# Router logits in four column groups, the routing chain in another order, the first expert weights split meanwhile, and another end of the program

## What is computed

```python
def moe_ffn(h, router, w1, w3, w2):
    shape = h.shape
    ht = h.reshape(-1, shape[-1])
    logits = (ht @ router).astype(jnp.float32)
    top_v, top_i = lax.top_k(logits, TOP_K)
    wts = jax.nn.softmax(top_v, axis=-1)
    combine = jnp.sum(jax.nn.one_hot(top_i, N_EXPERTS, dtype=jnp.float32) * wts[..., None], axis=1).astype(h.dtype)

    def expert_step(acc, p):
        e1, e3, e2, cw = p
        return acc + cw[:, None] * swiglu(ht, e1, e3, e2), None
    ...
# at the end of the layer:  x = x + gt2 * rms_norm(ffn(h), g_post_ffn[l])
```

## Time and profile before

| | |
|---|---|
| three timed executions | 2008.66, 2008.34 and 2004.48 us, median 2008.34 |
| the profiled execution's own time | 2004.63 us, its span 2002.5 us (2.1 us lie around the span) |
| TensorE | busy 94% of the span, mean granted clock 0.95 of full speed |
| VectorE, ScalarE, GpSimd | busy 62%, 53%, 2% |
| chain that ended last | TensorE 84%, VectorE 9%, ScalarE 3%, DMA 2%, issue 2% |
| the expert part | from about 1058 us to the end |

### The profile page before, as it was taken

One profiled execution on the slowest core, in us unless ns is written; L12 is line 12 of the kernel. 1 busy time (PEld: TensorE's weight loads), 2 busy tenths in 40 slices (PEclk: granted clock), 3 DMA queues, 4 the chain that ended last, 5 costly groups with the idle time before them and its releaser, 6 DMA issues.

```text
span 2002.5 us, 25665 instructions
## 1 busy us (share of the span) xinstructions
PE 1889.0 (94%) x10248; PEld 1547.4 (77%) x10248; DVE 1244.3 (62%) x1416; ACT 1071.2 (53%) x1432; POOL 32.0 (2%) x33
## 2 busy tenths in 40 slices
PE   6999879999999999998797999999999999999995
PEld 3877456898888787975586888888888888888783
DVE  3332751552232336434645989898888989898886
ACT  4323542462222226434436777767676777676764
POOL 0000000000000000000000110000000000000000
PEclk9999885899999999998877999999999999999997
DMA  8211643222322221414513999999989999998983
GB/s 345 101 48 70 234 159 127 83 69 102 105 84 105 85 106 50 147 64 183 218 64 145 368 351 361 348 360 347 360 344 355 351 342 365 337 371 335 355 335 148
DMA packets 61531, 441.87 MB, mean 221 GB/s; under 512 B 6836, under 2 KB 6964, under 8 KB 8288
## 3 DMA queue, kind: packets, MB, share of 16 engines
q1 hardware_dynamic: 60032, 436.23, 58.1%
q10 hardware_dynamic: 1120, 3.28, 0.4%
q0 software_dynamic: 256, 0.66, 0.1%
HBM read 439.10 MB, written 1.05 MB: 220 GB/s over the span
## 4 chain that ended last, share of the span: by engine, by line
PE 84%; DVE 9%; ACT 3%; DMA 2%; issue 2%; SPq 0%; ACTq 0%; DVEq 0%
PE psum L1610 73%; PE psum L2002 2%; DMA raw<-units 2%; PE psum L1849 1%; PE psum L1855 1%; PE psum L2045 1%; DVE row_max L1260 1%; PE psum L1627 1%; PE psum L2018 1%; ACT probs L870 1%; DVE w_lo L1116 1%; PE psum L1633 1%; DVE states L1291 1%; DVE act_lo L1180 1%; DVE probs L1254 1%
## 5 line engine op out<-in xcount | busy, mean ns | idle before, releaser
L1495 DVE TENSOR_TENSOR w_lo<-raw,w_hi 128x2048 fp32r<-128x2048 f32 x136 | 311.0, 2290 | 50.6 <-ACT w_hi L1014 49.9
L1014 ACT ACTIVATE w_hi<-raw 128x2048 fp32r<-128x2048 f32 x136 | 260.8, 1919 | 106.3 <-PE psum L1610 104.7
L1116 DVE TENSOR_TENSOR w_lo<-raw,w_hi 128x1024 fp32r<-128x1024 f32 x130 | 153.2, 1220 | 188.8 <-ACT w_hi L671 188.7
L1610 PE MATMUL psum<-w_hi,xt_hi 128*128 128x512 f32 x596 | 233.4, 392 | 2.7 <-DVE xt_lo L1500 2.7
L1610 PE MATMUL psum<-w_hi,xt_lo 128*128 128x512 f32 x596 | 232.7, 390 | 0.0
L1610 PE MATMUL psum<-w_lo,xt_hi 128*128 128x512 f32 x596 | 232.4, 390 | 0.0
L1495 DVE TENSOR_TENSOR w_lo<-raw_more,w_hi 128x2048 fp32r<-128x2048 f32 x90 | 206.0, 2290 | 34.5 <-ACT w_hi L1014 34.2
L1610 PE MATMUL psum<-act_hi,w_hi 128*128 128x512 f32 (+1 forms) x608 | 218.6, 359 | 1.4 <-DVE w_lo L1116 1.3
L1610 PE MATMUL psum<-act_hi,w_lo 128*128 128x512 f32 (+1 forms) x608 | 217.9, 358 | 0.0
L1610 PE MATMUL psum<-act_lo,w_hi 128*128 128x512 f32 (+1 forms) x608 | 217.9, 358 | 0.0
L1014 ACT ACTIVATE w_hi<-raw_more 128x2048 fp32r<-128x2048 f32 x90 | 172.7, 1919 | 74.4 <-PE psum L1610 74.4
(11 more groups left out here) (273 smaller groups left out, 3509.5 us busy)
## 6 DMA issues: line engine op xcount, KB each, us to landing
raw<-units SPq DMA_DIRECT2D x295, 1024.0 KB, 4.8
raw_more<-units SPq DMA_DIRECT2D x120, 1024.0 KB, 4.9
X<-ctx_in ACTq DMA_DIRECT2D x1, 1024.0 KB, 16.8
X<-x_in ACTq DMA_DIRECT2D x1, 1024.0 KB, 23.5
out<-X SPq DMA_DIRECT2D x1, 1024.0 KB, 4.1
const<-const_in ACTq DMA_DIRECT2D x1, 520.0 KB, 10.0
rope<-rope_in POOLq DMA_DIRECT2D x2, 256.0 KB, 5.4
wsm<-wsm_in ACTq DMA_DIRECT2D x1, 288.0 KB, 27.5
```

Of the source, the lines that this page charges most:

```text
L1014: act.activation(w_place(m)[0], raw_place(m), ACT.Copy).then_inc(esem("w_high"), 1)
L1116: ins = dve.tensor_tensor(w_lo[:, i % RING, part], raw[:, i % RING, part], w_hi[:, i % RING, part].bitcast(F32), ALU.subtract)
L1495: dve.tensor_tensor(lo, raw_place(m), hi.bitcast(F32), ALU.subtract).then_inc(esem("w_ready"), 1)
L1610: ins = pe.matmul(dst, lhs(a), rhs(b), start=first and n == 0, stop=last and n == 2)
```

## The change

Six things, all in the expert part:

1. The logits are made with the router's weights as the stationary operand (padded to 32 columns, in four column groups of the array, key `LR`); ScalarE copies the four partial sums, and a product with a 0/1 matrix (`C_SUM`) adds and turns them (`LG`). The router's weights in SBUF grow from 64 to 256 columns.
2. VectorE instead of ScalarE makes the last half tile of `h2T` (`last_half`), and its clearing of `y_moe` comes behind that. A one-element Exp on ScalarE (`warm`) stands ahead of the tokens' rounding.
3. VectorE makes two of the four lower parts of the tokens behind `routed`. ScalarE's copies of the gates move behind the split of unit 1, and its splits no longer wait for the places.
4. VectorE splits only units 0 and 1 ahead of the first gathered tokens, and ScalarE only 0, 1 and 2; the first up chunk waits for each half of the gathered tokens apart.
5. A down chunk makes all of its first 512 columns and then all of the second, and signals in between (`out_half`) in a pass's last chunk; `output` takes the halves apart. The last pass's `output` stands at the end of `run`, ahead of the `If`, and the split of the unit that is three beyond the run's end stands inside the `If`.
6. The end is made by halves of 512 columns on VectorE and ScalarE alone: `finish` squares and gates each half as soon as it is added, the root's function is loaded ahead, GpSimd's sum is gone, and the two tiles are stored apart.

```diff
-            out += [("LG",)] + [("H2", q) for q in range(4)] + [("GB", l, 1, 1, h) for h in range(2)] + [("POS",)]
+            out += [("LR",), ("H2", 0), ("LG",)] + [("H2", q) for q in range(1, 4)] + [("GB", l, 1, 1, h) for h in range(2)] + [("POS",)]
...
@@ sync @@
-        for t in token_tiles(1, "out"):
+        for n, t in enumerate(token_tiles(1, "out")):
             sp.wait_ge(x_added("ffn", 1, t), 1)
-        sp.dma_start(out[0].rearrange("(t p) d -> p t d", p=P), X[:, CTX // P:TILES, :]).then_inc(stored, 16)
-        sp.wait_ge(stored, 16)
+            sp.dma_start(out[0, n * P:(n + 1) * P, :], X[:, t, :]).then_inc(stored, 16)
+        sp.wait_ge(stored, 32)
...
@@ scalar @@
+        copy_out(("LR",), mod_row[:, :], bank(("LR",))[:, 0:256])
+        act.activation(warm[:, :], eps, ACT.Exp).then_inc(sem("exp_table"), 1)
         for q in range(4):
...
-        gates_on_all(1, 1, (1,))
         act.wait_ge(sem("top_gap"), 1)
         act.activation(rt[:, 4:6], rt[:, 4:6], ACT.Exp).then_inc(sem("top_exp"), 1)
-
-        wait_copied(act, ("POS",))
...
-            wait_used(act, ("down", p * FC + FC - 1))
             if p:
                 act.wait_ge(esem("scattered"), 4 * p)
             for h in range(2):
+                if h == 0:
+                    act.wait_ge(esem("out_half"), p + 1)
+                else:
+                    wait_used(act, ("down", p * FC + FC - 1))
...
-                if down is not None:
+                if down is not None and down != run_last(r):
                     high(ahead(("down", down)))
                 if c == GATHER_STEP and p + 1 < PASSES_OF:
                     columns_high(p + 1)
+            output(RUNS[r][-1])
...
                 act.wait_ge(sem("xn_mix1"), TILES)
+                columns_high(0)
             high(m)
-        columns_high(0)
+            if m == 1:
+                gates_on_all(1, 1, (1,))
         run(0)
+
+        def finish(p):
+
+            act.activation(std[:, 0:1], eps, ACT.Sqrt).then_inc(sem("root_table"), 1)
+            for n in range(4):
+                tt, h = divmod(n, 2)
+                act.wait_ge(esem("added"), 4 * p + n + 1)
+                if n >= 2:
+                    act.wait_ge(sem("final_square"), n - 1)
+                act.activation(y_junk[:, h * 512:(h + 1) * 512], y_moe[:, tt, h * 512:(h + 1) * 512], ACT.Square,
+                               accum_out=y_part[:, 2 + tt, h:h + 1]).then_inc(sem("final_square"), 1)
 
         def extra(k):
             with act.If(run_valid(act, k)):
+                high(RUN_END[k] + W_RING - 1)
                 run(k + 1)
...
@@ vector @@
+        tokens_low(0)
+        tokens_low(1)
         dve.wait_ge(sem("top_exp"), 1)
...
         dve.sem_inc(sem("routed"), 1)
+        tokens_low(2)
+        tokens_low(3)
...
-        for m in range(W_RING):
-            low(m)
+        low(0)
+        low(1)
         columns_low(0)
+        low(2)
+        low(3)
         run(0)
 
+        def gated_half(n):
+
+            tt, part = n // 2, slice((n % 2) * 512, (n % 2 + 1) * 512)
+            dve.wait_ge(sem("final_square"), n + 1)
+            dve.tensor_tensor(y_moe[:, tt, part], y_moe[:, tt, part], gate[:, 1, 1, part], ALU.mult).then_inc(
+                sem("final_gate"), 1)
+
         def finish(p):
-            output(p)
-            for n in range(4):
-                added(p, n, n)
-            dve.wait_ge(esem("added"), 4 * p + 4)
-            dve.sem_inc(sem("summed"), 1)
+            added(p, 0, 0)
+            added(p, 1, 1)
+            added(p, 2, 2)
+            dve.wait_ge(esem("added"), 4 * p + 4 - 1)
+            gated_half(0)
+            added(p, 3, 3)
+            gated_half(1)
...
+        tile_sum(0, 2)
+        gated_half(2)
+        tile_out(0, 2)
+        tile_sum(1, 3)
+        gated_half(3)
+        tile_out(1, 3)
...
@@ tensor @@
-        for tt in range(2):
-            for k in range(KT):
+        for k in range(KT):
+            for tt in range(2):
                 wait_copied(pe, ("TT", 1, "ffn", tt, k // 4))
-                ins = pe.matmul(bank(key)[:, tt * EXPERTS:(tt + 1) * EXPERTS], h2T(k)[:, tt * P:(tt + 1) * P],
-                                wsm[:, 512 + k * EXPERTS:512 + (k + 1) * EXPERTS], start=k == 0, stop=k == KT - 1)
+            group = slice(32 * (k % 4), 32 * (k % 4 + 1))
+            ins = pe.matmul(bank(key)[group, 0:LAT], wsm[:, 512 + 32 * k:512 + 32 * (k + 1)], h2T(k),
+                            start=k < 4, stop=k >= 4)
...
-            if c == 0:
-                pe.wait_ge(esem("xt_lo"), 2 * p + 2)
...
             for i in range(2):
+                if c == 0:
+                    pe.wait_ge(esem("xt_lo"), 2 * p + i + 1)
...
-            for j in range(2):
-                for h in range(2):
+            for h in range(2):
+                for j in range(2):
...
+                if c == FC - 1 and h == 0:
+                    ins.then_inc(esem("out_half"), 1)
```

More of the change, by code:

```diff
@@ L290 @@
 A_WSM = A_COLS + N_COLS
[L291 removed]
+WSM = 512 + 32 * KT
+A_GW2 = A_WSM + WSM
 A_AM = A_GW2
@@ L653, in _ @@
                     select(extra)
-        add(1, "ffn", y_moe_of)
     @block.scalar
@@ L800, in seam @@
                     tile_modulated(*after, n - 1, tiles[n - 1], (1,))
-            tile_modulated(*after, len(tiles) - 1, tiles[-1])
+            tile_modulated(*after, len(tiles) - 1, tiles[-1], (0,) if after == (1, "ffn") else (0, 1))
         def gate_logs(l):
@@ L1057, in run @@
                     high(ahead(("up", up, 0)))
-                    if c == (2 if p < EXPERTS else 0) and p:
+                    if c == 2 and 0 < p < EXPERTS:
                         output(p - 1)
@@ L1084, in extra @@
                 else:
-                    output(EXPERTS + k)
+                    finish(EXPERTS + k)
             with act.Else():
-                output(EXPERTS + k - 1)
+                finish(EXPERTS + k - 1)
         extra(0)
-        act.wait_ge(sem("summed"), 1)
-        mean_square("post", 1, "ffn", (2, 3), y_moe_of, lambda t: y_junk[:, :], lambda n: None)
+        for n, t in enumerate(token_tiles(1, "out")):
+            act.wait_ge(sem("final_sum"), n + 1)
+            act.activation(y_std[:, t:t + 1], y_ssq[:, t:t + 1], ACT.Sqrt, bias=eps, scale=1.0 / D_MODEL).then_inc(
+                sem("final_std"), 1)
     @block.vector
@@ L1371, in seam, with last_half @@
                     tile_low(*after, n - 1, tiles[n - 1], (1,))
+            if after == (1, "ffn"):
+                last_half(len(tiles) - 1, tiles[-1])
             tile_low(*after, len(tiles) - 1, tiles[-1])
+        def last_half(n, t):
+            key = ("TT", 1, "ffn", n, 1)
+            dve.wait_ge(sem("scale1"), 8)
+            dve.wait_ge(sem("turned_ffn1"), 2 * n + 2)
+            for k in range(4, KT):
+                ins = dve.tensor_scalar(h2T(k)[:, (t - 2) * P:(t - 1) * P], bank(key)[:, (k % 4) * P:(k % 4 + 1) * P],
+                                        modc[:, 1, 4, k, 1:2], modc[:, 1, 3, k, 1:2], ALU.mult, ALU.add)
+            empties(ins, key)
         def out_projection(l):
@@ L1467, in _, with tokens_low @@
         dve.tensor_tensor(field(TAKEN), field(FIRST), field(SECOND), ALU.add).then_inc(sem("taken"), 1)
-        for q in range(4):
+        def tokens_low(q):
             key = ("H2", q)
@@ L1974, in _ @@
             ins.then_inc(filled, 1)
+        tokens_back(0)
+        key = ("LG",)
+        wait_copied(pe, ("LR",))
+        wait_emptied(pe, key)
+        for tt in range(2):
+            ins = pe.matmul(bank(key)[:, tt * EXPERTS:(tt + 1) * EXPERTS], mod_row[:, tt * P:(tt + 1) * P],
+                            const[:, C_SUM:C_SUM + EXPERTS], start=True, stop=True)
+        ins.then_inc(filled, 1)
+        for q in range(1, 4):
+            tokens_back(q)
         gates_on_all(1, 1, (1,))
@@ L1986, in _ @@
         wait_copied(pe, ("POS",))
+        for q in range(4):
+            wait_copied(pe, ("H2", q))
         def gather(p):
```

37 lines of the change are left out of this document (22 added, 15 removed).

## The result

| | median of 4 timed executions | lowest to highest |
|---|---|---|
| before | 2006.41 us | 2003.92 to 2008.66 |
| after | 1984.89 us | 1981.62 to 1987.86 |

The ratio of after to before is 0.989, with a 95% interval of 0.987 to 0.991: faster, by 21.5 us. The forecast was 1992.0 us with a range of 1986 to 1998.

The account below looks back on a forecast made before the run. TensorE was taken as busy almost throughout, leaving gains only at the front and end: 7.2 + 7.7 - 0.3 = 14.6 us. That gave 1990.0 from the profiled execution, 1993.7 from the median; middle 1992.0, range 1986.0 to 1998.0.

Parts of the forecast that it names:

- selection earlier, behind the mark: Before the gather: `routed` at 1069.2 instead of 1073.96, 4.8 us earlier; the mark is the start of the last tile's turning.
- gather to first up product: Front: gather from 1071.1 at half clock throughout, with its two turnings, first up matmul at 1078.4; 7.3 us.
- more half clock in the up products: First up products: half clock may last somewhat longer since no pause precedes them; 0.5 us taken off.
- front: Everything ahead of the first up matmul: 7.2 us gained, after taking off 0.5.
- between: Expert passes: nothing from the new column order; 0.3 us lost to the router's padded weights in an early load.
- last down matmul to first sum: Kernel's end: first sum at 1981.6 instead of 1984.10, the `If` again costing 3.5 us; 2.5 us gained.
- end: Everything behind the last down matmul: 6.4 us from sums and finish plus 1.3 from the halved final store, 7.7 us.
- The second rival: Gather: the clock stays up through it, 3 to 4 us more gained, 1988.5 us; chance 0.2.
- the third rival: Kernel's end: the short branch over other `Else` bodies stalls like the long one, 3 us, 1995 us; chance 0.07.
- the clock rival: Gather: full clock kept through it, 3 to 4 us more gained, 1988.5 us, range down to 1986; chance 0.2.
- The GpSimd rival: Selection: VectorE's splits hold up GpSimd, `sel` 2.3 or 4.6 us later, 1994.3 to 1996.6 us; chance 0.25.
- the one on the order within down chunks: Down chunks: six matmuls in a row into one bank cost more, slower from 16 ns each; 2022 at 25 ns; chance 0.02.

Follow-up runs that it names:

- e1: The kernel before, unchanged, run again; ratio to before 0.9994 (0.9985 to 1.0002).
- e4: The kernel after, unchanged, run again; ratio to before 0.9895 (0.9877 to 0.9913).
- e6: The kernel after with VectorE's first split moved ahead of the tokens' last two lower parts, beside the selection; ratio to before 0.9931.
- e10: The kernel after with the product of a run's last up chunk ahead of the split of its second unit; ratio to before 0.9900.
- e11: The kernel after with the split that no pass uses back ahead of the last output and the `If`, on both engines; ratio to before 0.9905.
- e12: The kernel after with gates behind places and the product of a run's last up chunk ahead of the split; 1982.93 us, ratio to before 0.9889.
- e2: The kernel before with only the front of the change (items 1 to 4), the end as before; ratio to before 0.9944.
- e7: The kernel after with the last pass's output inside the `Else` and in the next run's start, not ahead of the `If`; ratio to before 0.9918.
- e8: The kernel after with four extra products of 256 columns, result unused, in TensorE's pause ahead of the gather; ratio to before 0.9895.
- e9: The kernel after with the gates' eight products moved behind the places' products on TensorE, into the pause before the gather; ratio to before 0.9904.

## Why the prediction was off

The sum was 14.6 us; the two totals give 20.0, and timed executions 20.2 (e1's median against e4's) to 22.0 (the median of all 17 executions of before on that chip against e4's). By its steps:

| step (bold: us gained) | predicted | measured | |
|---|---|---|---|
| selection earlier, behind the mark | 4.8 | 5.2 | logits 2.26 us where 2.0 were put; the chain behind a little shorter |
| gather to first up product | 7.3 us | 5.83 us | 1.5 us at full clock |
| more half clock in the up products | -0.5 | 0 | half clock in them: 2.9 us before, 2.5 after |
| **front** | 7.2 | 9.6 | |
| **between** | -0.3 | 0.4 | half of it by the up products' clock |
| last down matmul to first sum | 2.5 less | 3.7 less | 8.47 to 4.79 us |
| four sums | 4.55 us | 4.19 us | 4.59 before |
| last sum to `X` complete | 5.35 us | 4.71 us | 9.22 before |
| release of the store to the end | 3.3 us | 3.1 us | 4.59 before |
| **end** | 7.7 | 10.1 | |

**Front.** The step that failed is "It took 7.2 us with its two turnings, at half clock throughout; the last ends at about 1078.4": 5.83 us were measured. The second rival, the clock that stays up through the gather, happened in part. Against it stood that small products do not raise the clock; but it rose 9.0 us behind the mark, in the turnings back, and fell at 15.6 to 15.8 (after; e4, e6, e10, e11 and e12 alike). Before it rose at 12.1 and fell at 19.0, just ahead of the gather at 19.5. The change brought the gather to 14.3, in front of the fall. The prediction took the clock as a property of the gather, and the rival as all or nothing, so that its middle had no place in the forecast. Why the clock falls at that moment stays open: it fell at 14.8 in e2, at 13.0 in e7, and not at all in e8, and I found no rule in these rows that gives all of them. So part of this gain is luck of the execution: e7, with after's front unchanged, gained 8.7 us there and not 9.6, its gather at 13.9 being behind the fall. The rest of the front stood: 16 records of logits in 2.26 us, the table's load hidden beside the sum, no wait for the splits of units 2 and 3, the clearing of `y_moe` hidden.

**End.** The step that failed is "I put the same behind 1978.15": the `If`'s 3.5 us counted from the start of the instruction before it. The price was nearly right and the starting point was not. From the last rounding's end (1963.83) to the first instruction of the `Else` pass 3.66 us, 0.67 to the branch and 2.99 from there, where 3.5 were put; but they were counted from 2.52 us behind the last down matmul's start, and they ran from 1.03. The branch comes 0.67 us behind the last rounding of ScalarE that VectorE's queue waits for, here in the shadow of a split and of both lower parts (after, e7, e11). The trace of before has the same: ScalarE's rounding ahead of the unused split ended as VectorE began it, at 1978.0; the branch (line 1591) is at 1978.6, and `ey_lo` starts 2.9 us behind it, at 1981.49. This is 1.2 of the 2.4 us missed; the rest are small terms taken too high by 0.2 to 0.6 each. No run takes item 6 apart; what its steps are worth is read from the rows alone. The short branch over the other bodies cost nothing, so the third rival did not occur.

**Base.** I set the forecast midway between the profiled execution and the median. Both hold the clock's chance ahead of the mark, which moved it from 1053.3 to 1058.7 over 14 profiled executions. From the profiled execution the sum gave 1990.0, from the median 1993.7; 5.4 us more of gain make 1984.6 and 1988.3. With the fourth execution before, the median is 2006.41, and the sum from there 1991.8, so the choice of base is not what failed. The range's low end, 4 us below that first sum, allowed only for the clock rival, and not for an end mis-sized by 2.4 us beside it: without those 2.4 us the time would have been 1987.3, inside the range (an estimate).

The GpSimd rival did not occur, but e6 shows its price, 3.5 us, of which 2.1 are the selection and the rest the clock, and how near it was. Nothing came of the one on the order within down chunks: 36 matmuls in 8.21 us. Its threshold of 16 ns each is 19 us in all, 4 us more than both ends give; they would be used up at 12.5 ns (14.9 us over 1188 matmuls). The 1.28 us of VectorE's product alone are in the trace of before at 1991.86, not in the earlier trace rows.

## What to carry to other kernels

When a branch stands in a critical tail, count its stall from the last signal of another engine that its queue waits for, not from the engine's own backlog, and put work that is already released between that signal and the body (0.6 us here, after against e7). When a stage moves earlier, ask in which clock it will then run: read the moments at which the granted clock rose and fell against a mark, not only its value in the stage. And compare totals from a mark behind the unchanged part, since that part alone moved by 5 us here.

## What the runs showed of the hardware

- A branch to the far body costs VectorE's queue 2.83 to 3.04 us (after, e7, e11), but the queue reaches it while earlier work runs: in e7 1.64 us ahead of the end of the running split. It gets there 0.67 to 0.68 us behind the last signal that it waits for.
- GpSimd's two instructions of the selection, 1.58 us alone, took 3.72 us when VectorE's subtraction of two SBUF operands (2.29 us) began 0.03 us ahead of them (e6), and 5.79 us where two such subtractions stood back to back (after). The Trainium skill (GPSIMD Engine Reference, Specifications) names this contention for VectorE instructions with two SBUF inputs, and the traces agree: beside the tokens' lower parts, which read one operand from PSUM, the selection took its 1.58 us. The runs add the size, and that GpSimd waited where it began behind such a subtraction. VectorE beginning second waited beside GpSimd's sum (3.39 us for 1.28), but not in the last 0.39 us of the selection (after, 1067.27).
- TensorE waits 2.1 us at the ends of both runs in all 14 executions, and the granted clock fell to 0.50 behind that wait at some of them only: at the last end alone in 12 executions (before and after among them), at the first alone in e8, at both in e9. Why is open; each fall cost 1.6 to 1.7 us, as much as most edits of the last experiments.
